# Two-layer model on one core: four normed output stages turned to tokens on partitions, x updated token-major

## The chip, the cores and the metric

One NeuronCore of a Trainium2 chip. The time is device microseconds of one execution. The kernel keeps all activations in on-chip memory (SBUF) for the whole run and streams the weights once, in fp32.

## The reference, cut to what matters

A first block (NSA attention, retention, MLP) is followed by two layers; x is 512 tokens by 1024 features. What the change touches:

```
rms(y, g) = y * rsqrt(mean(y*y over features) + 1e-6) * g
layer 0:  y = mlstm(rms(x, pre0)) ;  x = x + rms(y @ w_out, post0)          # stage mout
          u = rms(x, ffn_pre0) @ w_up ; h = gelu(conv(u)) * conv(u)
          x = x + rms(h @ w_down, ffn_post0)                                # stages fd00, fd01, fd02
          k, v, f = split(rms(x, kv_norm) @ kv_w)                           # stages fk, ff, fv
layer 1:  q, g = split(rms(x, pre1) @ w_qg) ; o = fox(q,k,v,f) * sigmoid(g) # stages fg, fq
          x = x + rms(o @ w_out, post1)                                     # stage fout
          u = ... ; x = x + rms(h @ w_down, ffn_post1)                      # stages fu1x, fd1x ; x is the output
```

So there are four places where a product is normed, scaled by a gain and added to x, and after three of them x is normed again and multiplied at once with the next weights. "Seam" below is such a place: A is mout to fu00, B is fd02 to fk, C is fout to fu10, D is fd12 to the end of the kernel.

## The kernel before, in words

Every weight matrix passes as blocks of 128 x 2048 numbers (128 x 1536 in fd02 and fd12, whose inner width is 6 tiles of 128). A block is loaded by SyncE (`load`, L305), rounded to fp32r by ScalarE (`hi_part`, L356) and its remainder is taken by VectorE (`lo_part`, L371). Activations are split in the same way (`high` L684 on ScalarE, `low` L688 on VectorE), and a product is three fp32r matmuls: high by high, high by low, low by high (`three_products`, L427 to L429).

In `dense` (L470) the weights are the stationary operand, the activations stand with features on partitions (tiles of 128 features by 512 tokens), and the result has features on partitions too: a block of weights gives two such tiles, in 2 chunks x 8 input tiles x 3 = 48 matmuls of 512 columns. `by_tile` (L521) is the form for a stage whose input tiles come one by one: it waits for each input tile and works on both chunks; with `lag=1` it does blocks 0 and 1 together, one tile apart. In `dense_rows` (L579) the activations are stationary and the weights move, so that the result has tokens on partitions; a PE drain (L628) closes every second block.

`split_between` (L393) orders ScalarE and VectorE inside a stage: for each block `early`, then the rounding of the block after next, then `late`. `ahead_act` and `ahead_dve` are what the two do first in a stage.

The normed output stages (mout, fout, fd02, fd12) are `dense` with `sums_on_the_way` (L794): VectorE takes the two result tiles of a block out of PSUM, ScalarE squares them, VectorE adds the squares up in `total`. `post_root` (L843) then needs TensorE twice: `column_sums` (L669) sums over partitions by matmuls, ScalarE takes the root, VectorE the reciprocal, and `spread` (L677) brings it to all partitions in bank 6. `update_and_split` (L870) goes through the eight tiles: VectorE scales y by gain and root (L893), adds it to x (L903), ScalarE makes the high half (L684) and a square (L888), VectorE the low half (L688) and the running sum (L899); TensorE follows tile by tile with blocks 0 and 1 of the next stage, whose results are multiplied by the second root (`inv`) when they leave PSUM. At the end of the kernel `update_and_store` (L936) scales (L948), adds (L953, three of the eight on GpSimd) and stores eight tiles of 128 x 512. The result is stored feature-major and transposed on the host.

x is `xT[:, k, :]`, tile k of 128 features by 512 tokens.

Of the kernel before, what the change touches and what calls it, by code (L numbers as in the profile page):

```python
# [106 lines left out]
def weight_forms():  # L107
# [6 lines left out]
    f.update(mqk=(4, [(KT, 256)]), mg=(1, [(KT, 128)]), mv=(4, [(4, 512)]), mo=(4, [(4, 512)]), mout=(4, [(KT, 256)]))  # L114
    for l in range(2):
        if l == 1:
            f.update(fk=(4, [(KT, 256)]), ff=(1, [(KT, 128)]), fv=(4, [(4, 512)]), fg=(4, [(KT, 256)]), fq=(4, [(KT, 256)]),
                     fout=(4, [(KT, 256)]))
        for g, (f0, n) in enumerate(FG):
            f[f"fu{l}{g}"] = (n, [(KT, 256)])  # L120
            f[f"fd{l}{g}"] = (4, [(n, 256)])
# [3 lines left out]
def packed_weights(inputs):  # L125
# [15 lines left out]
    def rows(name, a, start, groups):  # L141
        columns(name, *[a[512 * q:512 * q + 512, start + 512 * g:start + 512 * g + 512] for g in range(groups) for q in range(2)])
# [26 lines left out]
    plain("mout", w["mlstm_w_out_2"][0], 0, 4)  # L169
    for l in range(2):  # L170
        up, down = w["ffn_w_up_2"][l], w["ffn_w_down_2"][l]
        for g, (f0, n) in enumerate(FG):
            columns(f"fu{l}{g}", *[cat(up[:, P * f:P * f + P], up[:, FF + P * f:FF + P * f + P]) for f in range(f0, f0 + n)])
            plain(f"fd{l}{g}", down[P * f0:P * (f0 + n)], 0, 4)
# [5 lines left out]
    plain("fout", w["fox_w_out_2"][0], 0, 4)  # L180
# [3 lines left out]
def build(nc, io, at):  # L184
    top = ExitStack()
    with top:
# [22 lines left out]
        sq, y_part = ([work4[:, 2 * n + r, :] for r in range(2)] for n in range(2))  # L209
        total = sb(top, "total", [P, S])  # L210
# [6 lines left out]
        part_col = sb(top, "part_col", [P, TT])  # L217
        conv = sb(top, "conv", [P, 4, 88])
# [62 lines left out]
        rotated, second_in = tally("rotated"), tally("second_in")  # L281
        stored = tally("stored")
# [92 lines left out]
        def marks():  # L375
            return {"slot": stream["slot"], "turn": stream["turn"], "eager": False, "crossed": False, "raw": [t.n for t in raw_loaded], "hi": hi_ready.n, "lo": lo_ready.n, "hi_half": hi_half_ready.n,
# [16 lines left out]
        def split_between(eng, spec, nxt, m, part, early, late, ahead, lag=None):  # L393
# [4 lines left out]
            if n > 4:  # L398
                if lag:
# [5 lines left out]
                with eng.Fori(1 if lag else 0, n // 2 - 1) as i:  # L405
# [6 lines left out]
            for b in range(first, n):  # L412
                early(eng, b, slot(b % 2), m)
                if m["eager"] and b == 2:
                    part(eng, spec, nxt, 5, 1, m)
                elif n > 1 and b + 2 <= n and not (lag and b == 0):
                    part(eng, spec, nxt, b + 2, b % 2, m)
                late(eng, b, slot(b % 2), m)
                if m["eager"] and b == 1:
                    part(eng, spec, nxt, 4, 0, m)  # L420
# [48 lines left out]

        def dense(name, chunks, early_dve=none, late_dve=none, early_act=none, late_act=none, tile_ready=None,  # L470
# [2371 lines left out]
```

## Time and profile before

| | |
|---|---|
| median of 3 runs | 2106.36 us (2105.05 to 2107.86) |
| the profiled execution: its time, its span | 2106.26 us, 2104.5 us |
| PE busy, share of the span | 2046.5 us, 97% |
| PE weight loads | 1658.8 us, 79% |
| DVE (VectorE) | 1227.9 us, 58% |
| ACT (ScalarE) | 791.7 us, 38% |
| granted TensorE clock, mean | 0.99 |
| chain that ended last | PE 86%, DVE 6%, PE weight loads 3% |

Times in rows are in us from the span's start; a form row gives count, busy us and mean ns. The end of a matmul is modelled: matmuls of 512 columns follow each other every 0.227 us although each row says 0.39 us. So the distance between starts is what a matmul takes, and "busy" overstates PE where it waits.

### The profile page before, as it was taken

To read this page: it belongs to the slowest core of one execution; us is meant where nothing else is said; L and a number is where in the kernel's file an instruction comes from. 1 tells how busy PE (TensorE), PEld (TensorE's weight loads), DVE (VectorE), ACT (ScalarE), POOL (GpSimd) and SP (SyncE) were. 2 spreads that over 40 slices of the span, in tenths; PEclk is the share of its full clock that TensorE was granted. 3 is DMA by queue.
4 is the path that set the end of the run, shared out by engine and by line. 5 is a ranking of instruction groups with operands and counts; after the bars stand their busy time and mean duration, and the time that the engine had idled before them with its cause. 6 is when DMAs were issued, how large, how long until landed. Compare 5 with 4: busy or idle time off the path is not lost.

```text
span 2104.5 us, 25495 instructions
## 1 busy us (share of the span) xinstructions
PE 2046.5 (97%) x9840; PEld 1658.8 (79%) x9848; DVE 1227.9 (58%) x1726; ACT 791.7 (38%) x1228; POOL 24.4 (1%) x45
## 2 busy tenths in 40 slices
PE   8999999999999999999899999999999999999997
PEld 6866778888888888877788888878786678888886
DVE  5778635454435355456675573774537767647475
ACT  4258243332222232245443342342426734324242
POOL 1000000000000000000000000000000000000000
PEclk9999999999999999999999999999999999999998
DMA  5410412322222222321122222222221022222221
GB/s 190 161 41 9 144 39 100 110 100 100 98 85 98 100 100 89 111 91 49 72 100 100 88 92 100 85 95 90 97 86 38 15 87 80 100 100 100 98 85 58
DMA packets 34320, 188.52 MB, mean 90 GB/s; under 512 B 4392, under 2 KB 8648, under 8 KB 14608
## 3 DMA queue, kind: packets, MB, share of 16 engines
q1 hardware_dynamic: 32448, 181.24, 24.2%
q0 software_dynamic: 1568, 5.65, 1.0%
q8 instruction: 62, 1.02, 0.2%
q10 hardware_dynamic: 208, 0.33, 0.1%
q14 instruction: 34, 0.28, 0.0%
HBM read 182.54 MB, written 2.11 MB: 88 GB/s over the span
## 4 chain that ended last, share of the span: by engine, by line
PE 86%; DVE 6%; PEld 3%; issue 2%; ACT 2%; DVEq 1%; PEldq 0%; DMA 0%; SPq 0%; ACTq 0%
PE bank L427 23%; PE bank L429 23%; PE bank L428 23%; PE bank L510 3%; PE bank L515 3%; PE bank L511 3%; PE bank L1242 2%; PE bank L1212 1%; PE bank L1229 1%; PEld bank L427 1%; PEld bank L429 1%; PEld bank L428 1%; PE bank L2250 1%; DVE xT L903 1%; DVE a_lo L688 1%
## 5 line engine op out<-in xcount | busy, mean ns | idle before, releaser
L356 ACT ACTIVATE w_hi<-w_raw 128x2048 fp32r<-128x2048 f32 (+3 forms) x168 | 307.7, 1832 | 760.6 <-PE bank L429 626.5
L427 PE MATMUL bank<-a_hi,w_hi 128*128 128x512 f32 x1376 | 538.6, 391 | 1.6 <-DVE w_lo L371 1.1
L429 PE MATMUL bank<-a_hi,w_lo 128*128 128x512 f32 x1376 | 535.6, 389 | 0.0
L428 PE MATMUL bank<-a_lo,w_hi 128*128 128x512 f32 x1376 | 535.5, 389 | 0.0
L371 DVE TENSOR_TENSOR w_lo<-w_raw,w_hi 128x2048 fp32r<-128x2048 f32 (+3 forms) x168 | 367.9, 2190 | 155.0 <-ACT w_hi L356 155.0
L427 PEld LDWEIGHTS bank<-a_hi,w_hi 128*128 128x128 f32 x1376 | 258.3, 188 | 56.5 <-issue 1.9
L429 PEld LDWEIGHTS bank<-a_hi,w_lo 128*128 128x128 f32 x1376 | 258.3, 188 | 53.8
L428 PEld LDWEIGHTS bank<-a_lo,w_hi 128*128 128x128 f32 x1376 | 258.4, 188 | 52.9
L427 PE MATMUL bank<-big_halves,w_hi 128*128 128x512 f32 x616 | 240.1, 390 | 0.5 <-DVE w_lo L371 0.3
L429 PE MATMUL bank<-big_halves,w_lo 128*128 128x512 f32 x616 | 239.7, 389 | 0.0
L428 PE MATMUL bank<-big_halves,w_hi 128*128 128x512 f32 x616 | 239.7, 389 | 0.0
L427 PEld LDWEIGHTS bank<-big_halves,w_hi 128*128 128x128 f32 x616 | 115.6, 188 | 25.6 <-DVE w_lo L371 1.7
L429 PEld LDWEIGHTS bank<-big_halves,w_lo 128*128 128x128 f32 x616 | 115.6, 188 | 24.2
L428 PEld LDWEIGHTS bank<-big_halves,w_hi 128*128 128x128 f32 x616 | 115.6, 188 | 23.9
L427 PE MATMUL bank<-w_hi,a_hi 128*128 128x512 f32 (+1 forms) x288 | 111.4, 387 | 2.9 <-issue 1.1
L429 PE MATMUL bank<-w_hi,a_lo 128*128 128x512 f32 (+1 forms) x288 | 109.1, 379 | 0.0
L428 PE MATMUL bank<-w_lo,a_hi 128*128 128x512 f32 (+1 forms) x288 | 109.0, 379 | 0.0
L2620 DVE SCALAR_TENSOR_TENSOR shared<-shared,conv 128x512 f32<-128x512 f32 x88 | 66.2, 752 | 12.8 <-issue 10.5
L510 PE MATMUL bank<-big_halves,w_hi 128*128 128x512 f32 x184 | 72.0, 391 | 0.0
L511 PE MATMUL bank<-big_halves,w_lo 128*128 128x512 f32 x184 | 71.6, 389 | 0.0
L427 PEld LDWEIGHTS bank<-w_hi,a_hi 128*128 128x128 f32 x288 | 54.0, 188 | 19.1 <-issue 7.1
L2596 ACT ACTIVATE shared<-shared 128x512 f32<-128x512 f32 x44 | 27.9, 634 | 105.9 <-DVE shared L2620 105.9
(350 smaller groups left out, 2436.2 us busy)
## 6 DMA issues: line engine op xcount, KB each, us to landing
w_raw<-in_w_fu SPq DMA_DIRECT2D x44, 1024.0 KB, 4.8
w_raw<-in_w_up SPq DMA_DIRECT2D x16, 1024.0 KB, 4.8
w_raw<-in_w_down SPq DMA_DIRECT2D x16, 1024.0 KB, 4.8
w_raw<-in_w_fd SPq DMA_DIRECT2D x16, 1024.0 KB, 4.8
w_raw<-in_w_fd SPq DMA_DIRECT2D x8, 768.0 KB, 4.2
w_raw<-in_w_rqk SPq DMA_DIRECT2D x4, 1024.0 KB, 5.2
w_raw<-in_w_rvg SPq DMA_DIRECT2D x4, 1024.0 KB, 4.8
w_raw<-in_w_gate SPq DMA_DIRECT2D x4, 1024.0 KB, 4.8
```

What stands on the lines that cost most here:

```text
L356: act.activation(dst[0][:, cols], raw[slot][:, cols], ACT.Copy).then_inc(hi_half_ready.sem if half == 0 else hi_ready.sem, 1)
L371: ins = dve.tensor_tensor(dst[1][:, cols], raw[slot][:, cols], dst[0][:, cols].bitcast(F32), ALU.subtract)
L427: pe.matmul(out, w[0], x[0], start=first, stop=False)
L428: pe.matmul(out, w[0], x[1], start=False, stop=False)
L429: return pe.matmul(out, w[1], x[0], start=False, stop=last)
L510: pe.matmul(bank[2 * slot + c][:, :], w[0], x[0], start=k == 0, stop=False)
L511: pe.matmul(bank[2 * slot + c][:, :], w[1], x[0], start=False, stop=False)
L515: last = pe.matmul(bank[2 * slot + c][:, :], weights(ring, col)[0], x[1], start=False, stop=final)
L688: dve.scalar_tensor_tensor(a_lo[:, k, :], xT[:, k, :], vec(k), a_hi[:, k, :].bitcast(F32), ALU.mult, ALU.subtract).then_inc(split_lo_done. ...
L1242: last = pe.matmul(out[rows, j * P:S], vals[:, j, rows], turned_keys(p, e, j), start=j == 0 and not (together and p == 1), stop=j == TT - ...
L2596: act.activation(z[slot][:, 0, :], z[slot][:, 0, :], ACT.Gelu_apprx_tanh).then_inc(gelu_ready.sem, 1)
L2620: dve.scalar_tensor_tensor(z[slot][:, c, :], u[slot][:, c, 0:S], tap(0, b, c), z[slot][:, c, :], ALU.mult, ALU.add).then_inc(part_used.sem, 1)
```

## The change

The four stages change their form: weights of mout, fout and all `fd` stages are packed as for `dense_rows` (activations stationary, 512 weight columns moving). fd00, fd01, fd10, fd11 become `dense_rows`, unrolled. mout, fout, fd02, fd12 become the new `rows_post`: group 0 is the first 512 output features for all 512 tokens, group 1 the other 512 features, first for token tiles 0 and 1 (pair 0), then for 2 and 3 (pair 1). x is kept with tokens on partitions (`rows_of`), first turned at mout by 32 PE transposes. Norm sums are `accum_out` of ScalarE squares. x is turned back for the next stage by matmuls with a diagonal of the reciprocal roots, one pair of token tiles at a time, and blocks 0 and 1 of the next stage are computed in halves of 256 tokens (`by_half`). The store is token-major. The core of the diff:

```diff
-    ... mout=(4, [(KT, 256)])) ; fout=(4, [(KT, 256)]) ; f[f"fd{l}{g}"] = (4, [(n, 256)])
+    ... mout=(4, [(4, 512)])) ; fout=(4, [(4, 512)]) ; f[f"fd{l}{g}"] = (4, [(n // 2, 512)])
@@ dense
+                def by_half():
+                    for pair in range(2):
+                        cols = slice(pair * S // 2, (pair + 1) * S // 2)
+                        if pair:
+                            halves["turn"](pe, pair)
+                        for n in range(2):
+                            slot, ring, sets = begin(n, n)
+                            ring = spare_w if n == 0 else ring
+                            if pair == 0:
+                                halves["free"](pe, n)
+                            for i, k in enumerate(halves["order"]):
...
+                                for c in range(len(sets)):
+                                    last = three_products(pe, bank[home(n, slot, m) + c][:, cols], ..., [a[:, cols] for a in x], first, final)
@@ rows_post
+            order = [0, 2, 4, 6, 1, 3, 5, 7]
+            def sync(sp):
+                for b in range(2, 4):
+                    sp.wait_ge(lo_ready.sem, m["lo"] + b - 1)
+                    load(sp, spec, b, (slot0 + b) % 2, 0)
+                sp.wait_ge(lo_ready.sem, m["lo"] + 3)
+                sp.dma_start(gain_row[:, :], io["post_gains"][post:post + 1, :].broadcast_to([P, D])).then_inc(gain_row_in.sem, 16)
...
+            def turn_rows(pe, pair):
+                for t in (2 * pair, 2 * pair + 1):
+                    pe.wait_ge(diag_ready.sem, b_dg + t + 1)
+                for p in range(4):
...
+                    for k in (2 * p, 2 * p + 1):
+                        for t in (2 * pair, 2 * pair + 1):
+                            last = pe.matmul(turn_banks[p][:, col:col + P], xT[:, k, t * P:(t + 1) * P], diag[:, t * P:(t + 1) * P], start=True, stop=True)
+                    last.then_inc(rows_turned.sem, 1)
+            def tensor(pe):
+                ...   # group 0: for b, for n (input tile), for t in range(4): products
+                for pair in range(2):
+                    for q in range(2):
+                        pe.wait_ge(lo_ready.sem, m["lo"] + q + 3)
+                        for t in (2 * pair, 2 * pair + 1):
+                            ...   # group 1
+                if not final:
+                    turn_rows(pe, 0)
+            def pre_sqrt(act, t):
+                act.wait_ge(x_updated.sem, b_xu + 2 * t + 2)
+                act.activation(work4[:, 1:3, :]..., rows_of(xT, t), ACT.Square, accum_out=x_squares[:, t:t + 1])
+                act.drain()
+                act.activation(inv_col[:, t:t + 1], x_squares[:, t:t + 1], ACT.Sqrt, ...)
+            def scalar(act):
+                ahead_act(act, lambda: part(1)); part(2)
+                if turn_x: copy_x_rows(act, 0); copy_x_rows(act, 1)
+                part(3)
+                act.activation(warm[:, :], one[:, :], ACT.Sqrt)
+                for t in range(TT): square(act, 0, t)
+                part(4)
+                square(act, 1, 0); post_sqrt(act, 0); square(act, 1, 1); post_sqrt(act, 1)
+                if not final: pre_sqrt(act, 0); pre_sqrt(act, 1); part(5)
+                square(act, 1, 2); post_sqrt(act, 2)
+                if final: square(act, 1, 3); post_sqrt(act, 3)
+            def next_act(act, part):
+                high_pair(act, 0); keep_pair(act, 0) if keep
+                square(act, 1, 3); post_sqrt(act, 3); pre_sqrt(act, 2); pre_sqrt(act, 3)
+                high_pair(act, 1) ...
+            def vector(dve):
+                ahead_dve(dve, lambda: part(1)); part(2); part(3)
+                for t in range(TT): take(dve, 0, t)            # only where add (fd02, fd12)
+                for t in range(TT): gained(dve, 0, t)
+                dve.tensor_scalar(part_col[:, :], y_squares[:, 0, :], ...)
+                part(4)
+                for t in range(2): take(dve, 1, t); gained(dve, 1, t); update(dve, t)
+                if not final: diagonal(dve, 0); diagonal(dve, 1)
+                take(dve, 1, 2); gained(dve, 1, 2)
+                if final: update(dve, 2); take(dve, 1, 3); gained(dve, 1, 3); update(dve, 3)
+            def next_dve(dve, part):
+                low_pair(dve, 0); lo_part(dve, spec, nxt, 5, 1, m); update(dve, 2)
+                take(dve, 1, 3); gained(dve, 1, 3); update(dve, 3); diagonal(dve, 2); diagonal(dve, 3)
+                low_pair(dve, 1); part(None, 2)
+            def store(sp):   # 8 DMAs, each waits for its update; rows of 4 x 128 numbers
+            def block_free(pe, n):
+                waits = y_taken if add else y_gained
+                pe.wait_ge(waits.sem, (b_yt if add else b_yg) + TT + 2 * n + 2)
@@ ffn
-  dense(f"fd{l}{g}", two_chunks(h_tiles[:n]), copy_to(y) if g == 0 else add_to(y), tile_ready=up_ready)
+  dense_rows(f"fd{l}{g}", evac_dve=rows_to(y, g > 0), xs=h_tiles[:n], tile_ready=up_ready)
```

The block is shortened: several bodies stand on one line, and `if`/`for` one-liners stand for blocks. `take` is an add of 128x512 (PSUM plus y), `gained` a multiply of 128x512 by the gain row, `update` a reciprocal of 128x1 and two scaled adds of 128x512 into x, `diagonal` a reciprocal and a multiply of 128x128, `high_pair` and `low_pair` eight instructions of 128x256 each that read PSUM, `keep_pair` four copies of 128x512 (only at seam B, where fg needs the normed x again). The results of fk, fu, ff and fv leave PSUM by plain copies instead of a multiply by `inv`; the sigmoid of fg reads PSUM directly. mout's input transposes stand after input tiles 0, 1, 2 instead of 0, 3, 4, and the x transposes after tiles 4 and 6. `update_and_split`, `post_root`, `sums_on_the_way` and `update_and_store` are gone.

## Rows read from the trace of the kernel before

**Rows 1.** The page, part 1: busy us of TensorE.
```profile
PE 2046.5 (97%) x9840; PEld 1658.8 (79%) x9848; DVE 1227.9 (58%) x1726; ACT 791.7 (38%) x1228; POOL 24.4 (1%) x45
```
**Rows 2.** The four seams as windows: stretch, length, busy, clock, DMA share, GB/s.
```profile
1025.10:1061.40 36.30, 30.47 (x137) 25.07 (x136) 26.21 (x39) 14.41 (x23) 0.00 (x0) 0.86 0.08 29
1399.20:1433.40 34.20, 29.30 (x137) 24.26 (x136) 25.45 (x38) 13.23 (x22) 0.00 (x0) 0.90 0.06 21
1716.00:1751.50 35.50, 30.26 (x138) 25.11 (x137) 26.20 (x39) 14.45 (x23) 0.00 (x0) 0.86 0.08 30
2089.20:2104.50 15.30, 3.19 (x25) 2.79 (x24) 9.23 (x15) 0.80 (x2) 4.93 (x3) 0.65 0.37 137
```
**Rows 3.** Timeline of PE at seam C: start, length, engine, line.
```profile
1715.13 0.39 PE L429 MATMUL bank<-a_hi,w_lo 128*128 128x512 f32 x1
...
1715.81 0.39 PE L429 MATMUL bank<-a_hi,w_lo 128*128 128x512 f32 x1
...
1751.50 0.39 PE L427 MATMUL bank<-a_hi,w_hi 128*128 128x512 f32 x1
```
**Rows 4.** The chain that ended last, in order of time, seam C.
```profile
1725.74 0.73 ACT a_hi L684
1726.50 0.75 DVE a_lo L688
```
**Rows 5.** Timeline of PE: narrow matmuls, four transposes (L2277), one spread (L680).
```profile
61.82 0.29 PE L428 MATMUL bank<-w_lo,a_hi 128*128 128x280 f32 x1
61.95 0.29 PE L429 MATMUL bank<-w_hi,a_lo 128*128 128x280 f32 x1
...
985.66 0.60 PE L2277 MATMUL bank<-const_sb,big 128*128 128x128 f32 x4
986.01 0.48 PE L510 MATMUL bank<-big_halves,w_hi 128*128 128x512 f32 x1
...
1402.33 1.16 PE L680 MATMUL bank<-const_sb,post_col 128*128 128x128 f32 x8 [0.48 <-DVE post_col L863]
```
**Rows 6.** Timeline of PE on both sides of a drain (L628), twice.
```profile
252.03 0.39 PE L429 MATMUL bank<-w_hi,a_lo 128*128 128x512 f32 x1
252.68 0.47 PE L427 MATMUL bank<-a_hi,w_hi 128*128 128x512 f32 x1 [0.26 <-issue]
...
1482.16 0.39 PE L429 MATMUL bank<-w_hi,a_lo 128*128 128x512 f32 x1
1483.26 0.49 PE L427 MATMUL bank<-w_hi,a_hi 128*128 128x512 f32 x1 [0.71 <-issue]
```
**Rows 7.** Groups by form on ScalarE and VectorE: count, busy us, mean ns, idle before.
```profile
L371 DVE TENSOR_TENSOR w_lo<-w_raw,w_hi 128x2048 fp32r<-128x2048 f32 x148 | 339.1, 2291 | 151.7 <-ACT w_hi L356 151.7
L371 DVE TENSOR_TENSOR w_lo<-w_raw,w_hi 128x1536 fp32r<-128x1536 f32 x8 | 14.1, 1759 | 2.8 <-ACT w_hi L356 2.8
L356 ACT ACTIVATE w_hi<-w_raw 128x1536 fp32r<-128x1536 f32 x8 | 11.9, 1485 | 18.5 <-PE bank L429 15.0 <-PE bank L515 3.6
L840 DVE TENSOR_TENSOR big<-bank,big 128x512 f32<-128x512 f32 x16 | 10.5, 687 | 16.0 <-PE bank L429 16.0
L2331 DVE SCALAR_TENSOR_TENSOR shared<-bank,work 128x256 f32<-128x256 f32 x4 | 1.7, 424 | 14.4 <-PE bank L2242 14.4
L888 ACT ACTIVATE work<-xT 128x512 f32<-128x512 f32 x21 | 12.9, 615 | 0.0
L2462 ACT ACTIVATION_READ_ACCUMULATOR total<-bank 128x1 f32 x32 | 7.3, 227 | 0.0
L1995 ACT ACTIVATE big_halves<-shared 128x1024 fp32r<-128x1024 f32 x16 | 16.8, 1049 | 39.7 <-DVE shared L1990 39.7
```
**Rows 8.** The end: timeline of VectorE; issues with count, size, us to landing.
```profile
2099.33 1.40 DVE L948 SCALAR_TENSOR_TENSOR work<-big,gains,bank 128x512 f32<-128x512 f32 x2
2100.65 1.29 DVE L953 TENSOR_TENSOR xT<-xT,work 128x512 f32<-128x512 f32 x2
...
out_x<-xT SPq DMA_DIRECT2D x8, 256.0 KB, 2.0
```

More of the change, by code:

```diff
@@ L141, in rows @@
     def rows(name, a, start, groups):
-        columns(name, *[a[512 * q:512 * q + 512, start + 512 * g:start + 512 * g + 512] for g in range(groups) for q in range(2)])
+        half = a.shape[0] // 2
+        columns(name, *[a[half * q:half * q + half, start + 512 * g:start + 512 * g + 512] for g in range(groups) for q in range(2)])
     def cat(*parts):
@@ L558, in first_pair @@
                         between[0, "end"](pe)
-                    if spec.blocks > 1 and not lag:
+                    if spec.blocks > 1:
                         by_chunk(1, 1, True)
-                own = tile_ready is not None or between
+                own = tile_ready is not None or between or halves is not None
                 if spec.blocks <= 2 or own:
@@ L628, in use @@
                         pe.drain().then_inc(products_done.sem, 1)
-                if spec.blocks == 2 or between:
+                if spec.blocks == 2 or between or tile_ready is not None:
                     for b in range(spec.blocks):
@@ new lines, in rows_of, with as_tiles, rows_to, evacuate @@
+        def rows_of(x, t, g=None):
+            first, last = (0, KT) if g is None else (g * KT // 2, (g + 1) * KT // 2)
+            return x[:, first:last, t * P:(t + 1) * P]
+        def as_tiles(out):
+            return out[:, :].rearrange("p (k j) -> p k j", j=P)
+        def rows_to(dst, add):
+            def evacuate(dve, g, t):
+                y = rows_of(dst, t, g)
+                if add:
+                    return dve.tensor_tensor(y, as_tiles(bank[4 + t]), y, ALU.add)
+                return dve.tensor_copy(y, as_tiles(bank[4 + t]))
+            return evacuate
@@ L2773, in fox @@
                 split_lo_done.n += KT
-                more, root = post_norm("fout", y, tile_ready=halves_ready(b_hi, b_lo))
+                more, begin = rows_post("fout", y, 1, a_tiles, halves_ready(b_hi, b_lo), 0, False, lambda k: gain(8, k))
                 b_out = out_ready.n
-                return stages + more, root, lambda pool: pool.wait_ge(out_ready.sem, b_out)
+                return stages + more, begin, lambda pool: pool.wait_ge(out_ready.sem, b_out)
         y = big_tiles(0)
@@ L2796, in build @@
             stages += more
-            more, root, free = mlstm(ctx, *sums, rows, spare)
+            more, begin, free = mlstm(ctx, *sums, rows, spare)
             stages += more
-            more, root = ffn(0, big_tiles(2), root, y, u, z, free)
+            more, begin = ffn(0, begin, y, u, z, free)
             stages += more
-            more, root, free = fox(y, root, [x[:, n, :] for x in spare for n in range(2)])
+            more, begin, free = fox(y, begin, [x[:, n, :] for x in spare for n in range(2)])
             stages += more
-            more, root = ffn(1, y, root, y, u, z, free)
-            run(*stages, *more, update_and_store(y, 10, root))
+            more, last = ffn(1, begin, y, u, z, free)
+            run(*stages, *more)
 _INS = ["x", "positions", "norm_mix", "w_in", "cmp_pos_k", "cmp_pos_v", "cmp_k_w1", "cmp_k_w2", "cmp_v_w1", "cmp_v_w2",
```

552 lines of the change are left out of this document (322 added, 230 removed).

## The prediction

> **What bounds the kernel now.** I read the page first. TensorE is busy for 97% of the span [rows 1], so elementwise work that is removed counts only where PE waits for it; the question is where the missing part lies. "Busy" overstates PE: three matmuls of 512 columns start within 0.68 us, 0.227 us each, while each row says 0.39 [rows 3]. So I measured the seams by starts. From the last product of fout to the first matmul of block 2 of fu10 the trace has 35.5 us [rows 3]; blocks 0 and 1 are 96 matmuls, 21.8 us. The windows of the four seams are 36.3, 34.2, 35.5 and 15.3 us [rows 2]. That is 14.5, 12.4 and 13.7 us of loss, plus a tail of 15.3 us without any product: 56 us in all, the most that this change can touch. The chain in order of time says why: low half, add, high half follow one another tile by tile on VectorE and ScalarE, 0.75 and 0.73 us each [rows 4]. The clock is part of it: 0.86, 0.90 and 0.86 [rows 2] mean 10.2, 6.8 and 9.9 us at 1.2 GHz, each after PE had stood still; otherwise it is 2.4 GHz.
>
> **The end of the kernel (seam D).** Before: 15.3 us after the last product. After: token tile 3 comes last. VectorE is still on tile 2: its y is done 9 matmuls (2.0 us) earlier, then take 0.69 [rows 7], square 0.62 + 0.23, gained 0.69, reciprocal and drain about 0.3, two updates 1.4 [rows 8]: it ends at +2.2. Then tile 3: take 0.7, square and accumulator read 0.85, gained 0.7, reciprocal 0.3, two updates 1.35: +6.1. Then the store: 256 KB landed in 2.0 us as 2 KB runs [rows 8]; now the runs are 512 B, which no row shows. I take 2.5, between 2.0 and 3.5. Sum 8.7, so **-6.6**, between -5.5 and -7.5.
>
> **Seam C.** E is the end of the last product. Is pair 0's diagonal ready then? G is the end of group 0; group 1 has 96 matmuls, 21.8 us. ScalarE: rounding of block 3 1.9 (extrapolated from 1.05 for 1024 columns and 1.49 for 1536 [rows 7]), a table load, four squares at 0.8, rounding of the next block 1.9: G+8.6; VectorE's remainder 2.29 [rows 7]: G+10.9. Tiles 0 and 1 take gained, reciprocal, updates, 2.4 us each: G+15.8; the second square of 1024 with read and root 1.7, diagonal 0.6: G+18.1. It is ready 3.7 us early, so no wait. Then PE: `turn_rows` has 16 products of 128 columns in fp32; a spread of four is x8 rows in about 0.9 us [rows 5], so 16 are 3.6. A half block is 48 matmuls of 256 columns. The nearest row has 280 columns and 0.13 us between starts [rows 5], against 0.227 for 512; taking off 24 columns gives 0.1175, so 5.64 us per half block and 22.6 for four, 0.8 more than now. Block 1 may start only when its PSUM bank is free (`block_free`): y of tile 3 must have been read, and on VectorE that is queued behind `low_pair` (eight of 0.42 [rows 7], paced by the turning: E+6.5), the remainder of a block (2.2: E+8.7), `update` (1.7) and `gained` 0.7: E+11.1. PE would be there at E+9.3: **a new wait of 1.8 us**. Behind it pair 1's diagonal is ready at about E+15, PE needs it at E+16.8: no wait. Sum: 11.1 + 5.6 + 3.6 + 11.3 = 31.6 instead of 35.5: **-3.9**.
>
> Here the page "VectorE: DVE Perf Modes" of the Trainium skill (section on the errata) speaks against the change: operations on SBUF pay a fixed latency per instruction, so many small tiles cost more. The trace agrees: 0.42 us for 256 columns against 0.69 for 512 [rows 7].
>
> **Seam A.** The same 31.6 instead of 36.3: -4.7. But x must be turned once: 32 transposes; four take 0.35 to 0.45 [rows 5], so +3.5, all on PE, which has no gap there to hide them. Each input tile now carries 12 matmuls instead of 6 before PE asks for the next, so a late tile is covered better; I give that nothing. **-1.2**.
>
> **Seam B.** Here the cover is too short. Group 1 of fd02 has only 72 matmuls (6 input tiles), 16.3 us, and `add` puts a take before every square. From G: rounding 1.49, remainder 1.76 [rows 7]: 3.4. Takes and squares interleave, ScalarE is through at 7.3 (0.62 + 0.23 each [rows 7]); rounding of fk's first block 1.9: 9.3; remainder 2.29: 11.6. Token tiles 0 and 1, one after the other: take 0.69, square 0.85, gained 0.69, reciprocal and drain 0.35, two updates 1.35: 3.95 each, 19.5. Square of 1024 1.05 + 0.23 [rows 7] and root 0.4: 21.2; diagonal 0.6: 21.8. PE arrives at 16.3: **a wait of 5.5 us**. Then 31.6 as at C (`keep_pair`, four copies, 2.6 us, lies beside VectorE's remainder of the next block). 37.1 instead of 34.2: +2.9. After 5.5 us of nothing I expect the clock at 1.2 GHz for some 5 us of work, as in each seam now: +2.6. **+5.5**, between -2.6 (no wait) and +9. The next late thing is `low_pair`.
>
> **The down projections.** The count of matmuls stays 192 per stage of 8 tiles, and both forms run at the same pitch. But `dense_rows` closes each group with a drain: fd00, fd01, fd10, fd11 have two each, 8 in all. The rows show 0.65 us from start to start around one at a stage's end and 1.10 around one where PE also branches back in a loop [rows 6]. The new stages are unrolled, so 0.65: 0.42 lost each, **+3.4**, between 0 and 7.0 (8 x 0.87). The remainder on VectorE goes after four evacuations, with 10.9 us of products over it: nothing.
>
> **At nothing:** copies instead of multiplies by `inv` (0.69 either way, beside products); fg's sigmoid from PSUM (10.9 us of cover per block); four gain-row DMAs on SyncE, 512 KB each, queued before the next weights, which have some 10 us to spare. If SyncE's cover were gone, each would cost the 3 to 4 us of a broadcast.
>
> **Sum:** -6.6 - 3.9 - 1.2 + 5.5 + 3.4 = -2.8. Against the profiled execution's 2106.3 (span 2104.5 and 1.8 around it; the median, 2106.4, is the same): **2103.5 us**.
>
> The rows have no matmul of exactly 256 columns. The table in the same section of that page of the Trainium skill gives one: max(60, 6 + columns) cycles at 2.4 GHz, 109 ns. By that, an estimate, each seam would be 1.6 us shorter and the kernel at 2098.7. For 512 columns the table gives 216 ns where the trace has 227 [rows 3]; where they differ I go by the rows.
>
> **Rivals.**
> (1) *The second wait costs the clock in all three seams (slower).* Place: `block_free` before block 1 of fu00, fk and fu10. VectorE's queue there is nine instructions long; if PE's standing still there lets its clock fall to 1.2 GHz, as it did in each seam now, and for 6.8 us, as long as in seam B now, all of it under work, that is 3.4 us in each of three seams, +10.2: 2113.7. For: the three rows of 0.86 to 0.90 [rows 2], and half-rate turning delays `low_pair` in turn. Against: 1.8 us is shorter than the standing still of the seams now. The Trainium skill, "TensorE: Matmul & The Clock Gate", part 1: the throttled state is the default and activity releases it; by that rule every such gap is a candidate. 15%.
> (2) *Seam B does not wait (faster).* If ScalarE's squares and the remainder of fk's block are through before pair 0 ends, the chain is ready near G+16: -5.5 - 2.6: 2095.4. For: six of my terms there are singles, and overlapped instructions run closer (1.40 for two of 0.74 [rows 8]). Against: the order on VectorE is fixed. 30%.
> (3) *The new row form eats what the seams give (no change).* Drains at 1.10 instead of 0.65 give +3.6: 2107.1. 10%.
> (4) The forecast, with waits near those above: 45%, own range 2099 to 2107.
>
> **How the numbers follow.** 0.2% is 4.2 us, about what a measurement here can tell. Faster: rival 2 and the lower third of the forecast's case, 0.43. Same: the rest of it and rival 3, 0.41. Slower: rival 1, 0.16. The range runs from rival 2 with drains that cost nothing (2095.4 - 3.4) to rival 1: 2092 to 2113.
>
> **What would show it.** Seam windows by starts: 31.6 at A and C, 37 at B, 8.7 at the end; PE waiting for `diag_ready` at B only, and for VectorE's read of y before block 1 at all three; 3.5 us of transposes in mout; eight gaps of 0.65 at the drains; 256-column matmuls 0.117 apart. A wait at B under 2 us, or waits in A and C before the turning, would prove the order of ScalarE and VectorE misread; a clock under 0.9 in A or C would mean rival 1.

## The result, and the profile after

The changed kernel takes 2115.36 us (median of 5 runs, 2114.86 to 2118.26) against 2106.36 us; the ratio is 1.005, interval 1.0036 to 1.0063. It is slower by 9 us. The forecast was 2103.5 us with a range to 2113, so the time lies outside the range, on its slow side. The profiled execution took 2118.26 us, the longest of the five.

The page of the changed kernel, to be read against [rows 1]:

```profile
span 2116.5 us, 26480 instructions
PE 2067.9 (98%) x10208; PEld 1680.6 (79%) x10216; DVE 1193.2 (56%) x1714; ACT 814.2 (38%) x1325; POOL 19.4 (1%) x42
```

TensorE is still what the kernel waits for. The windows of the four seams by starts, in the order A, B, C, end; they answer to [rows 2]:

```profile
core 0: us, PE busy (x) PEld busy (x) DVE busy (x) ACT busy (x) POOL busy (x), PEclk, DMA share, GB/s
1037.40:1068.92 31.52, 29.82 (x257) 29.64 (x256) 20.29 (x36) 15.53 (x30) 0.00 (x0) 1.00 0.19 68
1412.41:1449.76 37.35, 31.67 (x257) 31.37 (x257) 21.77 (x42) 21.23 (x45) 0.00 (x0) 0.95 0.13 42
1732.28:1763.79 31.51, 30.00 (x258) 29.83 (x256) 20.28 (x36) 15.54 (x30) 0.00 (x0) 1.00 0.19 68
2107.30:2116.50 9.20, 0.16 (x1) 0.00 (x0) 4.96 (x9) 1.56 (x6) 0.00 (x0) 0.67 0.49 146
```

The reader is to see that the seams are not where the time went: 31.5, 37.4, 31.5 and 9.2 us where 31.6, 37.1, 31.6 and 8.7 were forecast (at B another 2.6 for the clock), and 36.3, 34.2, 35.5 and 15.3 stood before. The granted clock stays at 2.4 GHz through A and C. The waits are the ones that were expected, too. Timeline of PE in the changed kernel, at `block_free` (A), at a drain inside a stage, and at B:

```profile
1046.32 0.28 PE L432 MATMUL bank<-a_hi,big_halves 128*128 128x256 f32 x1
1048.30 0.35 PE L430 MATMUL bank<-a_hi,w_hi 128*128 128x256 f32 x1 [1.70 <-issue]
...
1156.40 0.39 PE L432 MATMUL bank<-w_hi,big_halves 128*128 128x512 f32 x1
1157.05 0.47 PE L430 MATMUL bank<-w_hi,big_halves 128*128 128x512 f32 x1 [0.26 <-issue]
...
1412.18 0.39 PE L432 MATMUL bank<-w_hi,big_halves 128*128 128x512 f32 x1
1416.55 0.68 PE L916 MATMUL bank<-work,xT 128*128 128x128 f32 x4 [3.98 <-DVE work L1055]
```

So I took landmarks, the same instruction at the end of an unbroken stage in both traces, and watched how far apart they are. The changed kernel was 5.3 us behind at 294 us, 8.4 behind at 881 us, 16.3 behind at 1685 us and 12.0 at its end. Between 294 and 881 us the diff touches nothing that runs. (Of the 5.3 us before that, most is the clock: this profile has two stretches of 6.8 us at 1.2 GHz, from 100.0 and 144.4 us, that the profile of before lacks.) The rows by line of one tile name, first the changed kernel and then the one before (count, then minimum/median/maximum ns):

```profile
L430 PE MATMUL bank<-w_hi,big_halves x416: 393/394/502, 987.2 to 2106.6; 128*128 128x512 f32 x139
L430 PE MATMUL bank<-big_halves,w_hi x304: 394/394/502, 322.7 to 806.6; 128*128 128x512 f32 x152
L431 PE MATMUL bank<-big_halves,w_hi x304: 388/388/398, 323.0 to 806.8; 128*128 128x512 f32 x152
L432 PE MATMUL bank<-big_halves,w_lo x304: 392/392/397, 323.2 to 807.0; 128*128 128x512 f32 x152
```

```profile
L427 PE MATMUL bank<-big_halves,w_hi x616: 387/389/501, 317.5 to 2088.6; 128*128 128x512 f32 x154
L428 PE MATMUL bank<-big_halves,w_hi x616: 387/389/398, 317.7 to 2088.8; 128*128 128x512 f32 x154
L429 PE MATMUL bank<-big_halves,w_lo x616: 388/389/397, 317.9 to 2089.0; 128*128 128x512 f32 x154
```

In a name like `bank<-big_halves,w_hi` the first operand streams and the second is stationary. Matmuls that read a big buffer last up to 394 ns instead of 389. From start to start (mean over neighbouring starts 215 to 260 ns apart, "pitch" below) they are 229.1 ns apart where the big buffer streams and 233.3 where it is stationary; before it was 226.7 to 227.0, and nearly all products without a big buffer still are at 227. The 229.1 is a mean over the three products of a triple, which in themselves stand at 231.7, 226.1 and 229.2 ns (L430, L431, L432). The new small tiles `y_squares` (32 bytes per partition) and `x_squares` (16, rounded up to 32) are allocated ahead of the big buffers and move them by 64 bytes, from 132736 to 132800. That became the theory to test.

### The profile page after: what moved, and what is told of

The parts are those of the page before. It is cut to its first block, busy times and chain, and to the rows that moved or that the text cites. A ratio compares the mean times of both kernels' runs of the same rounds, so it can differ in the third digit from the quotient of the medians.

```text
span 2116.5 us, 26480 instructions
## 1 busy us (share of the span) xinstructions
PE 2067.9 (98%) x10208; PEld 1680.6 (79%) x10216; DVE 1193.2 (56%) x1714; ACT 814.2 (38%) x1325; POOL 19.4 (1%) x42
## 4 chain that ended last, share of the span: by engine, by line
PE 88%; DVE 4%; PEld 3%; ACT 2%; issue 2%; DVEq 1%; DMA 0%; PEldq 0%; SPq 0%; ACTq 0%
PE bank L430 25%; PE bank L432 24%; PE bank L431 24%; PE bank L1418 2%; PE bank L517 2%; PE bank L518 2%; PE bank L522 2%; PE bank L1388 1%; PE bank L1405 1%; PEld bank L432 1%; PEld bank L430 1%; PEld bank L431 1%; PE bank L916 1%; PE bank L2426 1%; DVE w_lo L378 1%
## 5 line engine op out<-in xcount | busy, mean ns | idle before, releaser
L430 PE MATMUL bank<-a_hi,w_hi 128*128 128x512 f32 (+1 forms) x1424 | 549.2, 386 | 8.3 <-issue 7.2
L432 PE MATMUL bank<-a_hi,w_lo 128*128 128x512 f32 (+1 forms) x1424 | 545.2, 383 | 0.0
L431 PE MATMUL bank<-a_lo,w_hi 128*128 128x512 f32 (+1 forms) x1424 | 545.0, 383 | 0.0
L430 PEld LDWEIGHTS bank<-a_hi,w_hi 128*128 128x128 f32 x1424 | 268.4, 188 | 63.4 <-issue 10.8
L432 PEld LDWEIGHTS bank<-a_hi,w_lo 128*128 128x128 f32 x1424 | 268.3, 188 | 52.7
L431 PEld LDWEIGHTS bank<-a_lo,w_hi 128*128 128x128 f32 x1424 | 268.5, 189 | 51.1
L430 PE MATMUL bank<-w_hi,big_halves 128*128 128x512 f32 x416 | 165.5, 398 | 1.0 <-issue 1.0
L431 PE MATMUL bank<-w_lo,big_halves 128*128 128x512 f32 x416 | 164.5, 395 | 0.0
L432 PE MATMUL bank<-w_hi,big_halves 128*128 128x512 f32 x416 | 164.4, 395 | 0.0
L430 PE MATMUL bank<-w_hi,a_hi 128*128 128x512 f32 (+1 forms) x352 | 136.4, 387 | 2.9 <-DVE big L1897 1.0
L432 PE MATMUL bank<-w_hi,a_lo 128*128 128x512 f32 (+1 forms) x352 | 133.9, 380 | 0.0
L431 PE MATMUL bank<-w_lo,a_hi 128*128 128x512 f32 (+1 forms) x352 | 133.9, 380 | 0.0
L430 PE MATMUL bank<-big_halves,w_hi 128*128 128x512 f32 x304 | 120.0, 395 | 0.1
L432 PE MATMUL bank<-big_halves,w_lo 128*128 128x512 f32 x304 | 119.2, 392 | 0.0
L431 PE MATMUL bank<-big_halves,w_hi 128*128 128x512 f32 x304 | 118.0, 388 | 0.0
L430 PEld LDWEIGHTS bank<-w_hi,big_halves 128*128 128x128 f32 x416 | 78.2, 188 | 21.6 <-issue 2.7
L432 PEld LDWEIGHTS bank<-w_hi,big_halves 128*128 128x128 f32 x416 | 78.2, 188 | 18.9
L431 PEld LDWEIGHTS bank<-w_lo,big_halves 128*128 128x128 f32 x416 | 78.2, 188 | 18.3
L430 PEld LDWEIGHTS bank<-w_hi,a_hi 128*128 128x128 f32 x352 | 66.1, 188 | 21.7 <-issue 7.3
L432 PEld LDWEIGHTS bank<-w_hi,a_lo 128*128 128x128 f32 x352 | 66.1, 188 | 12.7
```

The costliest lines, as they stand in the source:

```text
L430: pe.matmul(out, w[0], x[0], start=first, stop=False)
L431: pe.matmul(out, w[0], x[1], start=False, stop=False)
L432: return pe.matmul(out, w[1], x[0], start=False, stop=last)
```

## Experiments

All timed runs had kernels of before beside them on the same chip; the ratios are to those.

**e1: 64 more bytes.** The theory's first form was that the buffers must start at a multiple of 128.

```
         conv = sb(top, "conv", [P, 4, 88])
+        sb(top, "pad", [P, 16])
```

> The changed kernel with 64 unused bytes per partition added ahead of the big buffers, so that these start at a multiple of 128 bytes again, as in the kernel before (there 132736; changed 132800; here 132864). Theory A (placement): the 48 new bytes of row-sum columns moved every buffer behind them by 64 bytes, and TensorE reads the big buffers slower from there. In the trace of the changed kernel the matmuls of 512 columns start every 233.3 ns where a big buffer is the stationary side (1223 in the trace) and every 229.1 ns where it streams (1149), against 226.7 of the same operands in the kernel before. 1248 x 6.6 ns + 1149 x 2.4 ns = 8.2 + 2.8 = 11.0 us: about 2104.4 us, ratio to before 0.999, both pitches back at 226.7 ns. Theory B (the seams and the drains cost more than forecast, placement costs nothing): 2115.4 us, ratio 1.004 or more. Theory C (token rows as such are slower, since stationary activations load slower than stationary weights): the 233.3 ns stay, the 229.1 fall, 2112.6 us.

Measured: 2120.78 us, ratio 1.0061 (1.0047 to 1.0075). Slower still; all three theories missed. But the place matters, since 64 unused bytes cost 5.4 us: the pitches are 232.5 to 233.6 ns (means by pair of buffers), streaming and stationary alike.

**e2: the kernel before, with its buffers where the changed kernel has them.** The same line, in before.

> The kernel before with 64 unused bytes per partition added at the same place, so that its big buffers start where the changed kernel has them (132800). Theory A (placement): some 2390 matmuls of its trace stream from a big buffer at 226.7 ns; at 229.1 ns they cost 2390 x 2.4 ns = 5.7 us more: about 2112.1 us, ratio 1.0027. The down-projections lose 2.4 ns a matmul here and 6.6 ns in the changed kernel, since here the weights are the stationary side. Theories B and C: 2106.4 us, ratio 1.000.

Measured: 2113.99 us, ratio 1.0036 (1.0022 to 1.0049): +7.4 us, 5.7 forecast. An old kernel with not one instruction changed loses most of what the change lost. Streaming from a big buffer takes 229.0 ns; `bank<-a_hi,big_halves`, where it is stationary, 233.1. Rows of e2, for these two:

```profile
L428 PE MATMUL bank<-big_halves,w_hi x616: 392/394/501, 318.3 to 2095.7; 128*128 128x512 f32 x154
L511 PE MATMUL bank<-a_hi,big_halves x48: 388/398/767, 1037.5 to 1753.7; 128*128 128x512 f32 x48
```

**e3: other distances in one kernel.** The big buffers at 64, 96, 32 and 32 bytes past a multiple of 128.

```
-            big = [sb(same, f"big{i}", [P, n]) for i, n in enumerate(sizes)]
+            big = [(sb(same, f"big{i}", [P, n]), i < 2 and sb(same, f"pad{i}", [P, (8, 16)[i]]))[0] for i, n in enumerate(sizes)]
...
```

> The changed kernel with unused bytes between the big buffers: the first stays at 64 past a multiple of 128 bytes, the second (upper half of the hidden values) lies at 96 past it, the third (their lower half) and the fourth at 32 past it. Theory A1 (any start off a multiple of 128 is as bad as any other): the pitch stays 233.3 ns in the down-projections, about 2115.5 us. Theory A2 (a start off a multiple of 64 is worse): pitch above 236 ns for all three products of the down-projections, 2119 us or more. Theory B: pitches as in the changed kernel, 2115.4 us.

Measured: 2117.82 us in one run. Pitches in the down projections are 234.3, 229.8 and 229.7 ns for the three products, elsewhere 228.3 to 234. Neither A1 nor A2: no single threshold orders these. The first two of the three have the same stationary operand and streaming operands that lie a multiple of 256 bytes apart, and still differ by 4.5 ns.

**e5 and e4: the distance, not the address.** In e5 the two tiles are allocated after `one`, behind everything; in e4 the kernel before gets 64 bytes ahead of all its buffers.

```
 e5
-        y_squares, x_squares = sb(top, "y_squares", [P, 2, TT]), sb(top, "x_squares", [P, TT])
...
         one = sb(top, "one", [P, 1])
+        y_squares, x_squares = sb(top, "y_squares", [P, 2, TT]), sb(top, "x_squares", [P, TT])
 e4
+        sb(top, "pad", [P, 16])
         raw = [sb(top, f"w_raw{r}", [P, SLOT]) for r in range(2)]
```

> The changed kernel with its two new small tiles allocated after all the others, so that every buffer of the kernel before lies exactly where it lay there (big buffers from 132736, 99840 = 390 x 256 bytes behind the rounded weights). The two shifts so far were both slow (64 bytes: 229 and 233.3 ns a matmul; 128 bytes: 233 and 232.5), so a plain multiple of 128 bytes is not the rule. Theory D (the distance between a big buffer and the buffer that TensorE reads beside it decides, best at a multiple of 256 bytes): all pitches at 226.7 to 227.3 ns, 11.0 us less than the changed kernel's 2115.4, about 2104.4 us, ratio 0.999. Theory C (stationary activations out of a big buffer are slow by themselves): streaming operands at 226.7, the down-projections stay at 233 ns, about 2112.6 us, ratio 1.003. Theory B (seams): 2115.4 us.

> The kernel before with 64 unused bytes ahead of all its buffers: every buffer has moved by 64 bytes, and no distance between two of them has changed. Theory D (distances decide): 2106.5 us, ratio 1.000, all pitches 226.7 to 227.3 ns. Theory E (the address itself decides, 128 past a multiple of 256 being the good one): the big buffers lose what they lost when they alone were shifted (7.4 us), and the activations' and weights' other buffers lose besides: 2114 us or more, pitches from 229 ns.

Measured: e5 2106.70 us, ratio 1.0002 (0.9993 to 1.0011); e4 2105.89 us, ratio 1.0001 (0.9991 to 1.0011). Theory D holds in both. Moving one line gives back 8.7 us, and all pitches are at 226.6 to 227.7 ns. Rows of e5:

```profile
L430 PE MATMUL bank<-w_hi,big_halves x416: 387/389/497, 981.1 to 2094.6; 128*128 128x512 f32 x139
L430 PE MATMUL bank<-big_halves,w_hi x304: 388/389/497, 319.8 to 800.6; 128*128 128x512 f32 x152
```

One stretch shows it best. From the first product of block 2 of fu00 to the last of fd02, the timeline of PE in the changed kernel and then in e5:

```profile
1068.92 0.40 PE L430 MATMUL bank<-a_hi,w_hi 128*128 128x512 f32 x1
...
1412.18 0.39 PE L432 MATMUL bank<-w_hi,big_halves 128*128 128x512 f32 x1
```

```profile
1062.18 0.40 PE L430 MATMUL bank<-a_hi,w_hi 128*128 128x512 f32 x1
...
1402.29 0.39 PE L432 MATMUL bank<-w_hi,big_halves 128*128 128x512 f32 x1
```

343.26 us against 340.11: 3.15 us, in which 528 matmuls have a big buffer as the stationary side (6.0 ns each). The second layer gives 3.2 the same way, mout 0.9, the stretch from 294 to 881 us 3.1: 10.4 us in all. 1.3 of it comes back in the seams: 0.5 because PE, being later, waits less at B (3.98 against 4.45 us), and 0.3 in each of the three because products of 256 columns run faster there (see the last section). The 9.1 that is left agrees with the 8.7 between the medians. Another 2.9 us by which these two profiles differ lie ahead of 294 us, mostly at the stretches of 1.2 GHz (two of 6.8 us in the changed kernel, one of 3.4 in e5), and are no part of it.

**e12 and e11: which distances.** In e12 two small tiles of the kernel before move behind the big buffers (64 bytes fewer); in e11 a 256-byte tile of e5 does.

```
 e12
-        mean_of = sb(top, "mean_of", [P, 1])
-        final_pre = sb(top, "final_pre", [P, KT])
         one = sb(top, "one", [P, 1])
+        mean_of = sb(top, "mean_of", [P, 1])
+        final_pre = sb(top, "final_pre", [P, KT])
 e11
-        ident_b = sb(top, "ident_b", [P, P], BF16)
         one = sb(top, "one", [P, 1])
+        ident_b = sb(top, "ident_b", [P, P], BF16)
```

> The kernel before with two small tiles moved from ahead of the big buffers to behind them: these start 64 bytes earlier (132672), 192 bytes past a multiple of 256 from the weights. Theory D (any distance off a multiple of 256 costs, 64 too few like 64 too many): some 2390 matmuls at about 229 ns, 2112 to 2114 us, as with 64 bytes too many. Theory D3 (only a buffer that lies too far costs): 2106.4 us, 226.7 ns.

> The changed kernel in the placement of e5, with one 256-byte tile moved from ahead of the big buffers to behind them: these start 256 bytes earlier (132480), 389 x 256 bytes behind the rounded weights, an odd multiple more. Theory D1 (the distance counts modulo 256 bytes): pitches of the products with big buffers 226.7 to 227.3 ns, 2106.7 us. Theory D2 (modulo 512 bytes or more): 229 ns and above, 2115 us or more.

Measured: e11 2108.07 us in one run, pitches 226.6 to 227.2: D1 holds, 256 bytes less change nothing, so the distance counts modulo 256. e12 2122.81 us, 10 us more than expected. Theory D's sign is right and its size wrong: streaming from a big buffer now takes 233.3 ns, while the stationary one takes 229.6, e2's two numbers exchanged. Rows of e12:

```profile
L427 PE MATMUL bank<-big_halves,w_hi x616: 393/394/502, 318.8 to 2104.2; 128*128 128x512 f32 x154
L428 PE MATMUL bank<-big_halves,w_hi x616: 392/394/398, 319.0 to 2104.4; 128*128 128x512 f32 x154
```

Counted as streaming address minus stationary address, modulo 256, the products of 512 columns read (means by pair of buffers; the single products of a triple lie apart, at 64 in the changed kernel from 226.1 to 231.7):

| distance | where | ns from start to start |
|---|---|---|
| 0 | before, e4, e5, e11 | 226.6 to 227.3 |
| 64 | after and e2, big buffer streams; e12, it is stationary | 228.6 to 229.6 |
| 128 | e1, both ways | 232.5 to 233.6 |
| 192 | after and e2, big buffer is stationary; e12, it streams | 232.9 to 233.4 |

**e6, e7: the two waits.** With placement out of the way, e5 stands at 2106.7 and not at the forecast 2103.5. e6 shortens VectorE's chain, e7 issues the last tile early.

```
 e6, vector
-                part(4)
-                for t in range(2):
-                    take(dve, 1, t)
+                for t in range(2):
+                    take(dve, 1, t)
+                for t in range(2):
                     gained(dve, 1, t)
                     update(dve, t)
                 if not final:
                     diagonal(dve, 0)
                     diagonal(dve, 1)
+                    part(4)
 e7, scalar
                 post_sqrt(act, 2)
+                square(act, 1, 3)
 e7, next_act
-                square(act, 1, 3)
                 post_sqrt(act, 3)
 e7, vector
                 gained(dve, 1, 2)
+                if not final:
+                    take(dve, 1, 3)
+                    gained(dve, 1, 3)
 e7, next_dve
                 update(dve, 2)
-                take(dve, 1, 3)
-                gained(dve, 1, 3)
                 update(dve, 3)
```

> On the placement of e5 (2106.7 us): in the normed stages VectorE takes both tiles of the first pair one after the other and only then multiplies them, and rounds the next stage's first block of weights (2.29 us) behind the diagonals and not ahead of the first take. Theory 1 (the 4.84 us wait of PE at fd02 to fk is VectorE's serial chain alone: 2.29 us of rounding plus 2 x 0.79 us in which it waits for ScalarE's squares plus 0.76 us ahead of the rounding): 4.6 us shorter, wait of PE 0.2 to 0.6 us; at the end of the kernel the backlog falls from 2.8 to 1.6 us, since tile 2 is only ready at 2093.4: together -4.3 - 1.2 = 2101.2 us, ratio 0.9977. Theory 2 (the wait is set by ScalarE or by the products): wait 3 us or more, 2105 us. Theory 3 (the rounded weights come too late for the next stage's first block): the wait moves there, 2105 us.

> On the placement of e5 (2106.7 us): the last tile's take, square and gain product are issued ahead of the split of the first pair and not behind it. Theory 1 (PE's three waits of 1.69 us ahead of the second block of fu00, fk and fu10 are for the bank that this tile still holds): the waits at 1039.59 and 1732.42 go (2 x 1.46 us over a matmul's 0.23), the one at 1418.03 gives 0.8 us since the second pair's diagonals come next: -3.7 us, 2103.0 us, ratio 0.9983. Theory 2 (something else holds PE there, a semaphore's path or the second block's weights): waits stay, 2106.7 us. Theory 3 (the earlier square delays the first a_hi by its 0.8 us and PE waits there): gaps of 0.8 us behind the turned rows in three places, 2105.4 us.

Measured: e6 2099.97 us, ratio 0.9972 (0.9960 to 0.9983); e7 2102.69 us, ratio 0.9987 (0.9978 to 0.9996). In both, Theory 1. In e6 the wait ahead of the turned rows is gone, and 0.96 us of it comes back behind them. Timeline of PE in e5 and then in e6:

```profile
1407.13 5.44 PE L916 MATMUL bank<-work,xT 128*128 128x128 f32 x32 [4.45 <-DVE work L1055]
1412.32 0.36 PE L430 MATMUL bank<-a_hi,big_halves 128*128 128x256 f32 x1
```

```profile
1403.59 0.39 PE L432 MATMUL bank<-w_hi,big_halves 128*128 128x512 f32 x1
1403.87 3.81 PE L916 MATMUL bank<-work,xT 128*128 128x128 f32 x32
1408.64 0.35 PE L430 MATMUL bank<-a_hi,big_halves 128*128 128x256 f32 x1 [0.96 <-DVE a_lo L1061]
```

The turned rows last 5.44 us in e5, where the clock is at 1.2 GHz for 3.4 us from 1407.5 on, and 3.81 now at 1.00: the fall of the clock went with the wait. In e7 PE goes from block 0 to block 1 without a gap at all three places.

**e8, e9, e10: together, the drains, the rest of B.** e8 is e6 and e7, and tile 3 is taken ahead of `update(dve, 2)` at the end. e9 adds:

```
-                        pe.drain().then_inc(products_done.sem, 1)
+                        pe.matmul(bank[0][:, 0:1], ident, one[:, :], start=True, stop=True).then_inc(products_done.sem, 1)
```

e10 puts, after a down projection, the split of the first pair ahead of the squares and gain products of tiles 2 and 3:

```
 scalar
-                square(act, 1, 2)
-                post_sqrt(act, 2)
-                square(act, 1, 3)
+                if final or not add:
+                    square(act, 1, 2)
+                    post_sqrt(act, 2)
+                    square(act, 1, 3)
 next_act
                     keep_pair(act, 0)
+                if add:
+                    square(act, 1, 2)
+                    post_sqrt(act, 2)
+                    square(act, 1, 3)
 vector
-                gained(dve, 1, 2)
+                if final or not add:
+                    gained(dve, 1, 2)
                 if not final:
                     take(dve, 1, 3)
-                    gained(dve, 1, 3)
+                    if not add:
+                        gained(dve, 1, 3)
 next_dve
+                if add:
+                    gained(dve, 1, 2)
+                    gained(dve, 1, 3)
                 update(dve, 2)
```

> e6 and e7 together, and at the end of the kernel tile 3 is taken ahead of the update of tile 2. If their gains are on different stretches they add: -5.5 - 3.7, and the end of the kernel -0.7 more: 2096.8 us, ratio 0.9956. If the second pair's diagonals become what PE waits for after fk's first half, 0.7 us of it is lost: 2097.5 us.

> e8, and the drain of PE at the end of each output group of the row stages (8 in the down-projections, 6 in the other row stages) is replaced by a matmul of one column into an idle bank that raises the same semaphore. Theory 1 (a drain costs PE 0.42 us, the rest of its 0.65 us gap being a matmul's pitch, and the column matmul 0.1): 14 x 0.32 = 4.5 us less than e8: 2092.3 us, ratio 0.9935. Theory 2 (the gap is the semaphore's and the instruction fetch's, not the drain's): as e8, 2096.8 us.

> e9 (2094.2 us), and where the token rows come from the down-projection, ScalarE splits the first pair ahead of the squares of tiles 2 and 3, and VectorE takes both tiles, splits, and multiplies them only then. Theory 1 (the 3.23 us for which PE waits behind the turned rows of fd02 to fk come from the squares of tiles 2 and 3 and the two products ahead of the split): the first a_hi is issued at about 1400.2 and the first a_lo at about 1402.3 in e9's times, the gap falls to 0.3 us: -2.9 us, 2091.3 us, ratio 0.9928. Theory 2 (the work moved behind the split comes too late for the second pair's diagonals): PE waits 2 us or more ahead of the second pair's rows, 2093.5 us.

Measured: e8 2096.72 us, ratio 0.9960 (0.9946 to 0.9973); e9 2094.17 us, ratio 0.9942 (0.9928 to 0.9955); e10 2091.41 us, ratio 0.9927 (0.9914 to 0.9941). e8 came out as summed, but not quite for the reasons given: at B a wait of 2.95 us stands behind the turned rows, since the work that e7 moved ahead of the split meets the rounding that e6 put there; e10 takes that away. PE in e8 and then in e10:

```profile
1399.96 3.81 PE L916 MATMUL bank<-work,xT 128*128 128x128 f32 x32
1406.71 0.36 PE L430 MATMUL bank<-a_hi,big_halves 128*128 128x256 f32 x1 [2.95 <-DVE a_lo L1060]
```

```profile
1396.99 3.81 PE L916 MATMUL bank<-work,xT 128*128 128x128 f32 x32
1400.78 0.36 PE L430 MATMUL bank<-a_hi,big_halves 128*128 128x256 f32 x1
```

The drains of e9 gave 2.6 us of the expected 4.5 between the medians. The traces give more: from the last product of a group to the first of the next is 0.37 us instead of 0.65 inside a down projection, and at its end the change saves 0.48, with two narrow matmul instructions in place of each of 15 drains. Part of that is lost at B. The wait there is 2.95 us in both profiles, but only in e9 the clock is at 1.2 GHz behind it, for 6.8 us, and PE falls back by 2.6 us against e8:

```profile
1405.83 0.55 PE L430 MATMUL bank<-a_hi,big_halves 128*128 128x256 f32 x1 [2.95 <-DVE a_lo L1060]
1406.17 0.41 PE L431 MATMUL bank<-a_lo,big_halves 128*128 128x256 f32 x1
```

Of the timed executions with the same mean clock, 0.998, the one of e9 took 2092.13 us and the three of e8 2095.92 to 2096.72: 3.8 to 4.6 us, as forecast. So the medians of e8, e9 and e10 hold the clock's share too. The seams of e10 by starts:

```profile
1028.02:1058.18 30.16, 30.16 (x257) 30.16 (x256) 20.68 (x36) 15.54 (x30) 0.00 (x0) 1.00 0.22 82
1396.94:1427.44 30.50, 30.50 (x257) 30.34 (x257) 20.75 (x35) 18.09 (x38) 0.00 (x0) 1.00 0.26 87
1709.25:1739.42 30.17, 30.17 (x258) 30.17 (x257) 20.70 (x36) 15.54 (x30) 0.00 (x0) 1.00 0.23 82
2078.20:2085.80 7.60, 0.16 (x1) 0.00 (x0) 4.50 (x9) 1.02 (x3) 0.00 (x0) 0.65 0.49 139
```

PE is busy without a gap in three of four, at full clock. This is the profiled execution, 2087.65 us; three of the five took 2091.41 to 2091.99 at a mean clock of 0.995 or 0.996 instead of 0.998, and no profile shows where. By the medians e10 beats both kernels: 14.6 us less than before, 24 less than the change as it was made.

## Why the prediction was wrong, point by point

**The step that failed** stands under "The down projections": "both forms run at the same pitch". I took 0.227 us from rows in which no distance between two buffers was off, and never asked where the change puts its new tiles. The change's allocations were no part of my sum, not even as an edit costed at nothing. The missing term is 8.7 us by e5 (10.4 by the stretches of the trace). It alone carries the result from "the same" to slower and out of the range, and none of my rivals had it. Of the 11.9 us between forecast and result the other 3.2 are the differences of the table below, of both signs. The pitch itself is right: with the old placement the row form runs at 227.0 ns, which e5 shows on 1223 starts; "token rows are slower as such" (Theory C) fell.

What is left is judged on e5, whose placement is that of before. By landmarks in the two traces:

| step | forecast | e5 against before |
|---|---|---|
| transposes of x in mout | +3.5 | +3.0 |
| seam A, 36.3 to 31.6 | -4.7 | -4.6 |
| seam B, wait and half clock | +5.5 | +3.9 |
| seam C | -3.9 | -3.7 |
| down projections (drains) | +3.4 | +5.2 |
| end | -6.6 | -5.6 |
| ahead of all seams | 0 | +2.3 |
| sum | -2.8 | +0.5 |

- **Seams A and C.** Right in every part: no wait for the diagonal, turned rows 3.5 us, a gap for `block_free` where it was put (1.69 us from start to start in e5, so 1.57 over the 0.12 of its product, 1.8 forecast; 1.70 <-issue in the changed kernel). e7 shows its cause. A product of 256 columns starts every 0.120 us in e5 and not every 0.1175; that costs 0.5 us over 192 of them, and the shorter gap gives 0.2 back. The Trainium skill's table ("VectorE: DVE Perf Modes", errata) gives 109 ns for this width; no run here shows it, and the measured 114 to 120 decide.
- **Seam B.** The wait is there and VectorE's chain is its cause (e6), but it is 4.45 us, not 5.5, and the clock costs 1.7 us (the turned rows take 5.2 us in place of 3.5), not 2.6. I had pair 0's diagonal at G+21.8; my terms were rows one after the other, and overlapped instructions run closer, as rival 2 said.
- **Drains.** 0.65 us from start to start inside a stage, as forecast. At a stage's end it is 0.83 to 0.86, which I had no term for: four of each make 4.1 in place of 3.4. The other 1.1 of the 5.2 us are spread over the ffn stages, whose nearly 3000 matmuls start some 0.4 ns further apart on average than before; the cause of that was not looked for. (The gap of 0.55 between the first two blocks of fd02 and fd12 stands in the profile of before too, at 1374.03 and 2064.07, and costs nothing new.)
- **The end.** 9.7 us in e5 (9.2 in the changed kernel) and not 8.7. Two terms were too small. "It ends at +2.2" assumed that VectorE keeps up with PE (and its terms add up to 1.9). It does not; each tile is a serial chain of 3.64 us, in which VectorE stands still 0.79 us for ScalarE's square, and tile 3 is taken at +2.9 us after the last product in e5, at +2.45 in the changed kernel (probably since its slower products leave VectorE more time; that was not tested). And the store: the span ends 3.0 us after the last update in both, where I took 2.5. VectorE in the changed kernel, after its last product at 2107.07:

```profile
2109.75 0.68 DVE L1035 TENSOR_TENSOR big<-bank,big 128x512 f32<-128x512 f32 x1
2111.22 0.69 DVE L1039 TENSOR_TENSOR big<-big,gain_row 128x512 f32<-128x512 f32 x1 [0.79 <-ACT work L958]
2111.84 0.15 DVE L1044 RECIPROCAL post_col<-post_col 128x1 f32<-128x1 f32 x1
2112.06 1.42 DVE L1049 SCALAR_TENSOR_TENSOR xT<-big,post_col,xT 128x512 f32<-128x512 f32 x2
```

  From that take to the end of the updates it is 3.7 us, 3.9 forecast. The stores land 2.3 to 2.6 us after their issue, 512-byte runs included; the issue itself takes 0.37 us, for which I had nothing.
- **Ahead of all seams**, e5's profile is 2.3 us behind that of before. 1.7 of it is a stretch of 3.4 us at 1.2 GHz near 100 us which the profile of before lacks; others of these traces, of kernels of before too (e2, e4), have one at about 145 us. e7, whose code up to there is that of e5, has neither, so it differs from one execution to the next, and I leave it there.
- **Rival 1** (the clock falls at the three `block_free` waits) is out: 1.00 in A and C. By the Trainium skill, "TensorE: Matmul & The Clock Gate", part 1, such gaps were candidates; here gaps of 1.7 to 2.0 us from start to start left the clock alone and idle times of 4.0 and 4.45 us did not; one of 2.95 us left it alone in e8 and not in e9. **Rival 2** was half right, as said. **Rival 3** named the right stages, "the new row form eats what the seams give", with the wrong cause.

That the placement explains the whole of the 9 us between the two kernels rests on e5 and e2 together: the one takes it out of the new kernel, the other puts it into the old (7.4 us there, with fewer products of the slowest kind). In the rest, errors of both signs cancel in part, which is luck: B and its clock cost 1.6 us less than forecast, the down projections, the end and the time ahead of all seams 5.1 more.

## What to carry to other kernels

- A new tile, however small, moves all that is allocated behind it. Compare the distances between matmul starts in stages that the change does not touch; a step from 227 to 229 and 233 ns is worth 9 us here, and of the durations, 389 ns before, only some show it (394, 388, 392). Put small new tiles last, and keep the operands that TensorE reads together a multiple of 256 bytes apart.
- When PE waits on a chain of short VectorE and ScalarE steps, issue order is cheap to change: take the next tile while the other engine squares this one, and put rounding that nobody awaits behind the chain. By the medians that took 12.7 us of the 15.3 from e5 to e10, some of it by way of the clock, and not an instruction was removed for it.

## What the runs showed of the hardware that was not expected

- The distance between a product's streaming and stationary operand, modulo 256 bytes, sets its mean pitch: 226.7 ns at 0, 229 at 64, 233 at 128 and 192, for 512 columns of fp32r. Moving all buffers by 64 bytes changes nothing (e4). 192 rests on three kernels, the effect of 64 bytes less on one timed execution of e12, with hundreds of starts in it. The distance is not all: single products of a triple differ at one and the same distance (226.1 to 231.7 ns at 64 in the changed kernel; 234.3 and 229.8 at 160 in e3). What in the chip this comes from was not tried.
- With 256 columns it is the other way: products of 256 columns whose stationary side is a big buffer last 276 ns and start every 0.114 us at distance 192, against 283 and 0.120 at distance 0. This agrees with seam A, 31.5 us in the changed kernel and 31.8 in e5.
- A drain of PE costs some 0.42 us inside a stage (0.65 from start to start, less a pitch) and 0.60 at its end; a narrow matmul that raises the semaphore in its place costs less by 0.28 to 0.30 and by 0.48 us (traces of e8 and e9).
- The same idle time of 2.95 us of PE at the same place was followed by 6.8 us at 1.2 GHz in e9 and by none in e8.
